# Attention units in pairs on the two halves of the partitions, two pairs scored ahead

## The reference

```python
def token_mixer(...):                        # first block, each layer
    oa = neighbourhood_attention(qa, ka, va, na_rpb)      # 8 heads, table of biases
    ob = sliding_window_gqa(qb, kb, vb, swa_sink)         # 8 query heads, a sink per head
    gates = sigmoid(gl + gate_bias)
    merged = gates[:, :, 0] * (oa @ w_branch_na) + gates[:, :, 1] * (ob @ w_branch_swa)
...
def attend(q, k, v):                         # second block, 4 query heads, 2 key heads
    s = jnp.einsum('bqhgd,bkhd->bhgqk', qg, k) * ATTN_SCALE
    p = jax.nn.softmax(s, axis=-1)
    o = jnp.einsum('bhgqk,bkhd->bqhgd', p, v)
...
def conv_module(a, ...):                     # second block: 31 taps over the tokens
    glu = a[..., :W_CONV] * sigmoid(a[..., W_CONV:])
    y = conv(glu, dw_w) + dw_b
```

## Time and profile before

| what | value |
|---|---|
| median of 3 runs | 2968.57 us (2967.52 to 2970.8) |
| profiled execution, its own time | 2964.72 us |
| its span, first to last instruction | 2962.8 us |
| granted TensorE clock, mean | 0.956 |
| TensorE busy | 2642.4 us (89%) |
| VectorE busy | 1467.9 us (50%) |
| ScalarE busy | 905.2 us (31%) |
| GpSimd busy | 995.4 us (34%) |
| DMA, mean | 276 GB/s |
| granted clock from 148 to 222 us (first block's attention) | 1.00 |

### The profile page before, as it was taken

The page is one execution under the profiler, slowest core; times in us unless marked ns, Lnnn a source line. Parts: engine busy times, 40 slices in busy tenths (PEclk is TensorE's granted clock), DMA queues, the critical chain, the costliest instruction groups (busy, mean ns, idle before and its releaser), DMA issues.

```text
span 2962.8 us, 29652 instructions
## 1 busy us (share of the span) xinstructions
PE 2642.4 (89%) x9800; PEld 1755.1 (59%) x9800; DVE 1467.9 (50%) x3150; ACT 905.2 (31%) x2248; POOL 995.4 (34%) x1040
## 2 busy tenths in 40 slices
PE   7899888987988888998988889898888999989999
PEld 6467743533434445677545555565355788857888
DVE  1631557798876435323677777777546100172000
ACT  1241134445543222421444444422432200123000
POOL 0000267667677610001576665766700000000000
PEclk9899999999999998999999999999996999979999
DMA  6445699999999964455999999999941344422444
GB/s 253 153 153 188 265 378 410 410 410 409 378 409 410 411 267 151 152 189 191 375 409 411 411 411 410 411 411 412 411 156 41 119 152 156 142 71 86 147 151 156
DMA packets 187296, 817.50 MB, mean 276 GB/s; under 512 B 20592, under 2 KB 22656, under 8 KB 154128
## 3 DMA queue, kind: packets, MB, share of 16 engines
q0 software_dynamic: 148784, 549.31, 46.7%
q1 hardware_dynamic: 38368, 266.35, 24.4%
HBM read 814.54 MB, written 1.05 MB: 275 GB/s over the span
## 4 chain that ended last, share of the span: by engine, by line
PE 52%; DMA 21%; POOL 12%; DVE 6%; issue 6%; ACT 1%; DVEq 0%; SPq 0%; ACTq 0%; POOLq 0%
PE work L603 45%; DMA arena<-experts_down,arena 11%; DMA arena<-experts_up,arena 8%; POOL arena L561 6%; POOL arena L586 6%; PE acc L603 6%; DVE arena L1647 2%; DMA ring<-stream 1%; PE work L677 1%; DVE small L1493 0%; DVE mx L1505 0%; DVE arena L1504 0%; DMA c<-consts 0%; DVE arena L1523 0%; PE acc L677 0%
## 5 line engine op out<-in xcount | busy, mean ns | idle before, releaser
L603 PE MATMUL acc<-arena 128*128 128x512 f32 x1860 | 901.4, 620 | 191.6 <-DMA arena<-experts_up,arena 153.8
L1647 DVE SCALAR_TENSOR_TENSOR arena<-arena,acc 128x1024 f32<-128x1024 f32 x512 | 620.1, 1220 | 370.3 <-DMA arena<-experts_down,arena 356.1
L586 POOL DMA_INDIRECT arena<-experts_down,arena x512 | 494.0, 965 | 909.7 <-DVE arena L1631 661.5
L603 PE MATMUL work<-arena,ring 128*128 128x256 f32 x3460 | 762.9, 383 | 17.6 <-ACT arena L1423 14.5
L603 PEld LDWEIGHTS acc<-arena 128*128 128x128 f32 x1860 | 343.0, 195 | 677.6 <-issue 574.7
L603 PEld LDWEIGHTS work<-arena,ring 128*128 128x128 f32 x3460 | 663.2, 192 | 121.0 <-issue 24.6
L561 POOL DMA_INDIRECT arena<-experts_up,arena x512 | 494.1, 965 | 235.9 <-issue 146.6
L603 PE MATMUL work<-h,ring 128*128 128x256 f32 x1440 | 333.2, 391 | 9.9 <-issue 8.6
L603 PEld LDWEIGHTS work<-h,ring 128*128 128x128 f32 x1440 | 278.0, 196 | 62.8 <-issue 25.0
L1222 ACT ACTIVATE arena<-arena 128x2 f32<-128x2 f32 x256 | 51.9, 203 | 630.5 <-DVE arena L1647 414.8
L603 PE MATMUL work<-lent,ring 128*128 128x256 f32 x992 | 224.2, 379 | 0.0
(11 more groups left out here) (234 smaller groups left out, 1683.7 us busy)
## 6 DMA issues: line engine op xcount, KB each, us to landing
ring<-stream SPq DMA_DIRECT2D x252, 1024.0 KB, 4.9
arena<-experts_down,arena POOLq DMA_INDIRECT x512, 14.9
arena<-experts_up,arena POOLq DMA_INDIRECT x512, 15.0
arena<-na_bias POOLq DMA_DIRECT2D x2, 2048.0 KB, 15.1
arena<-consts POOLq DMA_DIRECT2D x1, 2392.0 KB, 20.9
lent<-consts POOLq DMA_DIRECT2D x2, 1024.0 KB, 16.6
arena<-consts POOLq DMA_DIRECT2D x1, 1816.0 KB, 11.6
x<-x_in SPq DMA_DIRECT2D x1, 1024.0 KB, 5.6
```

The source lines that it names most:

```text
L586: pool.indirect_dma_start(down[:, (l * PICKS + n) % ROWS, :], None, experts[2 * l], bass.IndirectOffsetOnAxis(ap=expert[:, n:n + 1], axis=0))\
L603: ins = nc.tensor.matmul(o, w, r, start=start, stop=stop, **kw)
L1647: ins = v.scalar_tensor_tensor(row, row, 1.0, tok, ALU.mult, ALU.mult, accum_out=dot[:, n:n + 1])
```

## The change

Units go in pairs, (0, 1), (2, 3) and so on. `attention_order` gives steps of pairs: two pairs are scored first, then for each pair p: T(p), S(p+2), G(p), O(p), each for both units. Inside S and O the matmuls of the two units are issued alternately. `units2` reorders the second block's units so that the two of a pair lie on different partition halves. VectorE scores four units first, then normalises a pair, scores the pair two ahead, and runs six taps. ScalarE runs the exponentials of a pair ahead of the copies of the pair before it. Buffers for probabilities hold six units. In the second block the feature groups of the convolution come first, the head norms go behind group 8 and behind 28 taps, and 12 more taps follow them.

```diff
-TOKEN_FM = (0, 1, 2, 5, 6, 7, 8, 3, 4)
-NORMS_AFTER = 5
-TAPS_FIRST = 30
-TAPS_UNIT = -(-(2 * CONV - TAPS_FIRST) // 8)
+TOKEN_FM = (5, 6, 7, 8, 0, 1, 2, 3, 4)
+NORMS_AFTER = 8
+TAPS_FIRST, TAPS_NEXT = 28, 12
+TAPS_PAIR = -(-(2 * CONV - TAPS_FIRST - TAPS_NEXT) // 4)
+PAIRS_AHEAD = 2
+PROBS = 2 * (PAIRS_AHEAD + 1)
...
+def attention_order(pairs):
+    steps = [("S", p) for p in range(PAIRS_AHEAD)]
+    for p in range(pairs):
+        steps.append(("T", p))
+        if p + PAIRS_AHEAD < pairs:
+            steps.append(("S", p + PAIRS_AHEAD))
+        steps.append(("G", p))
+        steps.append(("O", p))
+    return steps
...
@@ units2
-            for s in range(4):
+            for i in range(4 * TT):
+                s = 2 * (i // (2 * TT)) + i % 2
+                t = i // 2 % TT
...
@@ TensorE, attention
                     if kind == "S":
+                        banks = [bank(f"{name}S", u) for u in pair]
                         for g in range(nq):
-                            mm(b[:, g * nk:(g + 1) * nk], un["q"][g], un["k"],
-                               inc=bank_full if g == nq - 1 else None)
+                            for u, b in zip(pair, banks):
+                                mm(b[:, g * nk:(g + 1) * nk], units[u]["q"][g], units[u]["k"],
+                                   inc=bank_full if g == nq - 1 else None)
...
+                        banks = [bank(f"{name}O", u) for u in pair]
+                        for u in pair:
+                            copied(pe, f"{name}T", u)
                         for kt in range(nk // P):
+                            for u, b in zip(pair, banks):
+                                base = units[u]["base"]
+                                mm(b[base:base + HD, 0:nq * P], units[u]["v"][kt],
...
@@ ScalarE, attention
-                exps(0)
-                for u, un in enumerate(units):
-                    if u + 1 < len(units):
-                        exps(u + 1)
...
+                for u in range(2):
+                    exps(u)
+                for p in range(len(units) // 2):
+                    pair = (2 * p, 2 * p + 1)
+                    for u in pair:
+                        if u + 2 < len(units):
+                            exps(u + 2)
+                    for u in pair:
+                        b = A.full(f"{name}T", u)
+                        A.free(f(prob_t_[:, u % 2, :], b[:, :], ACT.Copy), f"{name}T", u)
+                    for u in pair if beside else ():
+                        b = A.full(beside, u)
+                        A.free(f(gates[:, u, :], b[:, 0:T], ACT.Copy), beside, u)
+                    for u in pair:
...
@@ VectorE, attention
-                score(0)
-                for u in range(len(units)):
-                    if u + 1 < len(units):
-                        score(u + 1)
-                    normalise(u)
+                for u in range(2 * PAIRS_AHEAD):
+                    score(u)
+                for p in range(len(units) // 2):
+                    for u in (2 * p, 2 * p + 1):
+                        normalise(u)
+                    for u in (2 * p, 2 * p + 1):
+                        if u + 2 * PAIRS_AHEAD < len(units):
+                            score(u + 2 * PAIRS_AHEAD)
                     if taps:
-                        for _ in range(TAPS_UNIT):
+                        for _ in range(TAPS_PAIR):
                             next(taps, None)
```

More of the change, by code:

```diff
@@ L211, in attention @@
     def attention(name, units, beside=None):
[L212 to L220, removed]
+        for kind, p in attention_order(units // 2):
+            if kind != "G":
+                add(name + kind, 2)
+            elif beside:
+                add(beside, 2)
     for l in range(DEPTH):
@@ L683, in attention @@
                 copied(pe, *ready[2:])
-                for kind, u in attention_order(len(units)):
+                for kind, p in attention_order(len(units) // 2):
+                    pair = (2 * p, 2 * p + 1)
                     if kind == "G":
-                        if beside:
+                        for u in pair if beside else ():
                             group(bank(beside, u)[:, 0:T], KD, lambda k: h1[:, k, :], True)
@@ L698, in attention @@
                     elif kind == "T":
[L699 to L705, removed]
-                    else:
-                        copied(pe, f"{name}T", u)
-                        base = un["base"]
+                        for u in pair:
+                            b = bank(f"{name}T", u)
+                            pe.wait_ge(sem(f"{name}_prob"), u + 1)
+                            for g in range(nq):
+                                for kt in range(nk // P):
+                                    transpose_to(b[:, (kt * nq + g) * P:(kt * nq + g + 1) * P],
+                                                 prob_[:, u % PROBS, g * nk + kt * P:g * nk + (kt + 1) * P],
+                                                 k1("ident"),
+                                                 bank_full if (g == nq - 1 and kt == nk // P - 1) else None)
+                    else:
+                        banks = [bank(f"{name}O", u) for u in pair]
+                        for u in pair:
+                            copied(pe, f"{name}T", u)
@@ L1142, in exps @@
                                f"{name}_exp")
[L1143 to L1150 removed]
+                for u in range(2):
+                    exps(u)
+                for p in range(len(units) // 2):
+                    pair = (2 * p, 2 * p + 1)
+                    for u in pair:
[4 more added lines that the diff above has]
+                        A.free(f(prob_t_[:, u % 2, :], b[:, :], ACT.Copy), f"{name}T", u)
+                    for u in pair if beside else ():
                         b = A.full(beside, u)
                         A.free(f(gates[:, u, :], b[:, 0:T], ACT.Copy), beside, u)
[L1153 to L1154 removed]
+                    for u in pair:
+                        base, nq = units[u]["base"], len(units[u]["q"])
+                        b = A.full(f"{name}O", u)
+                        A.free(f(units[u]["o"], b[base:base + HD, 0:nq * P], ACT.Copy), f"{name}O", u)
             A.need("c1_loaded", 16)
@@ L1824, in _ @@
                 normalise_tokens(f"norm2_{l}", gs1, f"hs2_{l}")
-                for j in range(3):
-                    copied(dve, f"hn2_{l}", j)
-                    V.step(v.reciprocal(rs2[:, j, :], rs2[:, j, :]))
-                    o = key2[:, T:2 * T] if j == 2 else raw2[:, j, :]
-                    V.step(stt(o, o, k2("g_k" if j == 2 else "g_q", l), rs2[:, j, :]), f"qk_normed2_{l}")
                 V.need("glu_zero", 1)
@@ L1850, in _ @@
                 for _ in range(TAPS_FIRST):
+                    next(taps)
+                for j in range(3):
+                    copied(dve, f"hn2_{l}", j)
+                    V.step(v.reciprocal(rs2[:, j, :], rs2[:, j, :]))
+                    o = key2[:, T:2 * T] if j == 2 else raw2[:, j, :]
+                    V.step(stt(o, o, k2("g_k" if j == 2 else "g_q", l), rs2[:, j, :]), f"qk_normed2_{l}")
+                for _ in range(TAPS_NEXT):
                     next(taps)
```

51 lines of the change are left out of this document (16 added, 35 removed).

## The result

The changed kernel takes 2932.7 us (median of 4 runs, 2927.81 to 2934.66) against 2969.48 us (4 runs, 2967.52 to 2970.8) of the kernel before on the same chip: 0.9874 of the time, interval 0.9857 to 0.9891. That is some 37 us faster. The forecast was 2963, and the range ended at 2951.

A forecast was written before the change was run, and what follows sets the result against it. TensorE's own queue was taken as the bound (89% busy), in second-block attention a loop through TensorE and VectorE. First block -3.2, second -14.4, clock +12.2 gave -5.4 us off the median 2968.57: 2963, range 2951 to 2975.

The forecast's parts named there:

- Wider buffers for six units cost no instruction: Second-block step: enlarging the buffers to hold six units was said to cost no instruction; no time was put on it.
- Both overlaps: First block: a pair on two halves costs what one unit did, scores 1.06 us, value products 1.01 us.
- The stalls: First block: TensorE stands 2.15 us, or 3.45 with sinks, before a pair's first gate group, until ScalarE copies the transposes.
- The clock holds: Rival 2: no clock loss behind the first block's stalls, so -17.6 us, 2951; chance 0.17.
- a long fall behind each: Upper bound for clock loss behind the first block's ten stalls, 24 us; as rival 3, slower, +6.4, 2975; chance 0.12.
- 11.3, 11.3 and 4.5 us from pair to pair: Second block's attention: VectorE's time per pair, within a stage of 37.2 us against 44.45, 7.2 us gained per layer.
- The reorder ahead of it: Before second-block attention: moving features, norms and taps costs nothing, takes 5 us of taps out of the loop; cover 0.7 us.
- The forecast of 0.50 for the clock: Second block's attention: TensorE's granted clock stays at the low level, 0.50, throughout.
- Value products do overlap: Denies rival 4, value products don't overlap: 13 us over 16 pairs, about 3.6 in the second block, 2980; chance 0.07.
- Scores of a pair run one after the other: Rival 5, second block: a pair's scores don't overlap, +2 for each of four waits, 2971; chance 0.04.
- the falls of the clock: First block: lower granted clock behind the ten stalls of both layers, 12.2 us lost together, bounds 0 and 24.
- VectorE's wait in the second: Second block's attention: VectorE stands 3.5 us until the pair two ahead is scored, with the six taps behind.

## Why the prediction was right and where it was wrong

**The step that failed** is "Wider buffers for six units cost no instruction", and with it a sum that had terms for the attention stages alone. It is true that they cost no instruction. They moved the place where the gathered rows land by 128 bytes, and with them at the new place the expert stages became 27.4 us shorter in the profiled executions, and the kernel 28 to 29 by the two runs that shift or unshift alone. The prediction had priced this step at nothing without asking where the tensors behind the buffers would lie. With that term the forecast of 2963 would have been 2935; measured were 2932.7.

**First block.** Both overlaps hold: scores 1.14 for 1.13, values 1.08 for 1.08, where only the first had a row before. The stalls were worked out as 2.15 and 3.45 us, and are 1.94 and 3.24. Counted from the start of the transposes the bank came free after 4.17 and 5.47 us, where the sum had 4.2 and 5.5; most of the 0.2 is TensorE, which had its scores done after 2.2 us and not 2.08. They stand four and six times in the two layers, and the last two pairs have none, as forecast. By the sum the stage would be 1.6 us shorter and lose 6.1 to the clock, +4.5 in a layer; it was +3.8 and +2.5.

**The clock.** Six of ten stalls were followed by a fall, 11.2 us in all where 12.2 were taken. The rivals "The clock holds" and "a long fall behind each" both fail, by rows. TensorE: Matmul & The Clock Gate in the Trainium skill, HAM oscillation, describes kernels in which idle gaps between bursts of matmuls send the clock down again and again. This trace agrees for six stalls and not for the four behind which the window shows 1.00. Length alone does not part them: of two stalls of 1.94 us the one before 140.83 was followed by a fall, the one before 156.00 was not. That is not chance from run to run: in both layers of all six profiles that have these stalls the first was followed by a fall and the second was not. What parts them was not tried.

**Second block.** Forecast 11.3, 11.3 and 4.5 us from pair to pair, measured 11.09, 11.28 and 4.69. The stage came out at -6.3 and -7.0 for -7.2 each. The reorder ahead of it was put at nothing, and that holds: the stretch ahead is 1.7 us longer in layer 0, but the kernel before with the shift alone, which has no reorder, has the same 1.7, and the changed kernel without the shift has none. It is one fall of the clock that some executions have. The forecast of 0.50 for the clock was not met everywhere, and the times from pair to pair came out all the same: from 2232.30 to 2255.57 it was 0.65 on average.

```profile
2232.30:2255.57 23.27, 10.70 (x57) 6.59 (x57) 16.57 (x37) 7.33 (x17) 0.00 (x0) 0.65 0.13 46
```

**The rivals.** Value products do overlap, so that one falls. "Scores of a pair run one after the other" had been priced at +2 for each of four waits; with both units of a pair on one half it cost 0.2 to 0.5 us in a layer, and VectorE's waits were no longer than 3.48. The price assumed that VectorE waits for the scores of both units; it waits for the first unit's alone.

**The change proper.** -5.4 forecast, -7.2 measured, with an interval of the ratio (0.9969 to 0.9988) that spans 3.6 to 9.2 us. Direction and size of its parts hold. That the sum came out near this is in part luck: it rests on the falls of the clock, 12.2 us taken and 11.2 found, for which the rows gave anything from 0 to 24. What the change left behind is also what the prediction had pointed to without following it up: the first block's stalls, and VectorE's wait in the second. Removing both gave 51.7 us, more than the change and the shift together. TensorEngine Tiling (Array Packing), Performance Considerations, in the Trainium skill, names emptying PSUM as what may come to limit tiled matmuls. The trace agrees as to where the wait is; the run with the copies first shows that here the order of ScalarE's work made it, and not its throughput.

**Left open.** Why writes of gathered rows at an odd multiple of 128 bytes, or 64 bytes beside it, are slower was not shown, only that it is their address. Why the second chip gains so little of it was not tried either, nor was the order of copies or taps in the kernel before, without the pairs.

## What to carry to other kernels

When a change resizes any tensor, compare where the targets of the large transfers lie before and after; here 128 bytes were worth four times the change itself on the first chip, and the rate in the gather stage, 410 or 420 GB/s, tells it at a glance. When units are grouped, the work that frees a bank must go ahead of the work that is merely early: list what the draining engine has in its queue between a result and its copy. And where an engine waits for work two steps ahead, put independent work into that wait, not behind it.

## What the hardware showed

- The start of the gathered rows in a partition: 420 GB/s at multiples of 256 and of 512, 410 to 411 at an odd multiple of 128 and at 64 bytes from one, for rows that land in 12.8 or 14.9 us; 28 us of 2969 on one chip, about 5 on another.
- Matmuls of two units on different halves overlap when issued one unit behind the other: 8 records in 1.03 us against 1.01. With four matmuls to a unit alternate issue is the faster at a granted clock of 0.50, 1.98 us against 2.85 for 16 records.
- A stall of 1.94 us was followed by a fall of the clock once (0.83 over 10 us) and not another time (1.00), in the same stage and with the same work behind it, and so in both layers of six profiles.
